# Experts' gate and up products as seven block products of halves, side by side in column halves of TensorE

## The chip, the cores and the metric

The kernel runs on one core of one Trainium2 chip. The metric is the device time of one execution in microseconds; a median of several runs is given. All data is float32. TensorE, VectorE (DVE), ScalarE (ACT), GpSimd (POOL) and SyncE (SP, here the issuer of most DMAs) run side by side and wait for each other by semaphores.

## What is computed

The network has two blocks; the second one has two layers, and each layer ends in a mixture of experts. Only that part is touched:

```python
def ec_moe(h, w_router, w_gate, w_up, w_down):
    n, d = h.shape[1], h.shape[2]
    cap = max(1, EC_FACTOR * n // N_EXPERTS)
    aff = jax.nn.softmax((h @ w_router).astype(jnp.float32), axis=-1)
    gate, idx = lax.top_k(jnp.swapaxes(aff, 1, 2), cap)
    xe = jax.vmap(lambda hb, ib: hb[ib])(h, idx)
    hid = jax.nn.silu(jnp.einsum('becd,edf->becf', xe, w_gate)) * jnp.einsum('becd,edf->becf', xe, w_up)
    ye = jnp.einsum('becf,efd->becd', hid, w_down) * gate[..., None].astype(h.dtype)
    return jax.vmap(lambda yb, ib: jnp.zeros((n, d), yb.dtype).at[ib.reshape(-1)].add(yb.reshape(-1, d)))(ye, idx)
```

n = 1024 tokens, d = f = 1024, 16 experts, cap = 128: each expert picks 128 tokens, so all its products are 128 x 1024 by 1024 x 1024. There are 16 experts in each of two layers, 32 in all, each with 12.6 MB of weights that are used once.

## The kernel before

P = 128, KD = 8 (blocks of 128 along d), BANK = 512 (the columns of one PSUM bank of float32). `ffn` sets up a layer's experts: `stage_route` makes the lists of tokens, and while it runs SyncE loads the first expert's gate and up weights (`ahead`). `stage_moe` then goes over the experts, two in one turn of a loop; `e` is the expert and `q` its parity.

One expert in `stage_moe`. GpSimd gathers the 128 rows of x by an indirect DMA into `xg[q]`, two experts ahead. TensorE turns them by eight transposes (`turn_x`, L2645) into PSUM banks 0 and 1, and VectorE and ScalarE write half of them each, scaled and shifted, to `xT` (`evac_x`, L2724 and L2696). TensorE makes gate and up in two column halves of 512: four products of 8 k steps (L2663), into banks 2 to 5; `xT[:, k, :]` is the stationary operand, the weights move. A float32 matmul appears as two LDWEIGHTS and two MATMUL instructions in the trace, so 32 of them are 64 rows. ScalarE takes Silu of a gate half (L2704), VectorE multiplies the up half onto it (L2737, to `sg`). TensorE turns h by eight transposes (`turn_h`, L2651); VectorE copies one half (L2739) and ScalarE the other (L2708) to `hT`. The turn of the next expert's x stands between the two halves of h. Then come two down products of 8 k steps (L2679) into banks 6 and 7; VectorE scales them (L2749) into `ye[q]`, and GpSimd adds them to the rows of `xacc` by an indirect DMA (L2637).

The order on each engine is written out by hand; each works its list strictly in order. SyncE's list loads six weight blocks of 2 MB an expert (L2601), each into its only buffer as soon as the product that read it is done: gate and up halves, then the down halves. So at any time the transfers run one expert ahead of TensorE.

What the prediction's steps touch elsewhere: the router's product (L2497) with two tiles of 32 columns, attention's value product (L3916) with two tiles of 64 columns, and the stages that already work by the seven products (`SEVEN`; L2291, L2840, L3082), whose sums VectorE makes.

## Time and profile before

| | us |
|---|---|
| median of 3 runs | 4650.78 |
| lowest, highest | 4643.99, 4653.27 |
| the profiled execution's own time | 4645.05 |
| its span, first to last instruction | 4643.3 |
| TensorE busy | 4159.4 |
| VectorE busy | 1900.6 |
| mean granted TensorE clock (share of full speed) | 0.949 |

In the rows below PE is a TensorE matmul, PEld a TensorE weight load. A timeline row has the start in us from the span's beginning, the length in us, and the number of instructions merged in it (x64); their last one ends with the row. Behind it may stand how long the engine was idle before and what ended that. "128*64 128x512" is a matmul with 128 rows and 64 columns of stationary operand and 512 moving columns. PEclk is the granted clock: 1.00 is 2.4 GHz, 0.50 is 1.2 GHz. In groups by line the numbers are: busy us in total, mean ns of one, then the idle time before them and what ended it.

### The profile page before, as it was taken

What the parts mean: (1) busy time and instruction counts of PE and PEld (TensorE: products, weight loads), DVE (VectorE), ACT (ScalarE), POOL (GpSimd) and SP (SyncE); (2) the same over time, 40 slices, a digit from 0 to 9 for tenths busy, and PEclk for the clock granted to TensorE, in tenths of its full rate; (3) what the DMA queues carried; (4) which work ended last, traced back from release to release, by engine and by line L of the source; (5) the groups of instructions that cost most, each with busy time, mean ns of one, the idle gap of its engine ahead of it and who ended that gap; (6) DMA issues with size and microseconds to landing.
All of it is one profiled execution on the core that took longest, in us unless ns stands there. A gap on an engine that the chain in (4) does not pass through costs nothing. (4 is left out here: it accounts for less than half of the span.)

```text
span 4643.3 us, 37101 instructions
## 1 busy us (share of the span) xinstructions
PE 4159.4 (90%) x13298; PEld 2120.7 (46%) x13298; DVE 1900.6 (41%) x3452; ACT 1011.0 (22%) x1952; POOL 361.5 (8%) x349
## 2 busy tenths in 40 slices
PE   8999998988889699785849999998999995999996
PEld 3444444683444454445424444444444542444442
DVE  3556555445757333455761111115656564111111
ACT  3434452343020311272120000003210111000001
POOL 1011010200000000182000000000000000000000
PEclk9999999999999899898879999998999997999998
DMA  5121216447444222007239999952011115999985
GB/s 113 53 64 65 72 57 206 142 118 249 146 149 154 65 69 69 5 1 206 63 133 362 316 314 322 317 193 91 25 50 70 50 39 221 342 315 324 317 310 195
DMA packets 524366, 739.72 MB, mean 159 GB/s; under 512 B 127574, under 2 KB 233910, under 8 KB 524216
## 3 DMA queue, kind: packets, MB, share of 16 engines
q1 hardware_dynamic: 499272, 687.45, 43.9%
q0 software_dynamic: 11744, 43.00, 3.3%
q10 hardware_dynamic: 13200, 7.34, 0.5%
q8 instruction: 86, 1.41, 0.1%
q14 instruction: 64, 0.52, 0.0%
HBM read 660.65 MB, written 77.06 MB: 159 GB/s over the span
## 5 line engine op out<-in xcount | busy, mean ns | idle before, releaser
L2663 PE MATMUL ps<-ffn_w,moe_xT 128*128 128x512 f32 x2048 | 888.6, 594 | 3.3 <-DVE moe_xT L2724 3.3
L2663 PEld LDWEIGHTS ps<-ffn_w,moe_xT 128*128 128x128 f32 x2048 | 390.7, 191 | 495.5 <-issue 491.5
L507 PE MATMUL ps<-hT,pr_w 128*128 128x512 f32 x1344 | 588.6, 595 | 5.1 <-issue 3.8
L2679 PE MATMUL ps<-moe_w,moe_hT 128*128 128x512 f32 x1024 | 444.9, 592 | 0.1
L507 PEld LDWEIGHTS ps<-hT,pr_w 128*128 128x128 f32 x1344 | 254.3, 191 | 319.7 <-issue 316.8
L2737 DVE TENSOR_TENSOR moe_sg<-moe_sg,ps 128x512 f32<-128x512 f32 x64 | 44.0, 688 | 837.7 <-PE ps L2663 837.7
L2679 PEld LDWEIGHTS ps<-moe_w,moe_hT 128*128 128x128 f32 x1024 | 192.1, 190 | 230.1 <-issue 230.1
L2704 ACT ACTIVATE moe_sg<-ps 128x512 f32<-128x512 f32 x64 | 38.2, 597 | 1008.0 <-PE ps L2663 1008.0
L3326 PE MATMUL ps<-hA,abp_w 128*128 128x512 f32 (+1 forms) x624 | 252.3, 565 | 0.6 <-DVE bv L3439 0.6
L2749 DVE SCALAR_TENSOR_TENSOR moe_ye<-ps,moe_gc,moe_gt 128x512 f32<-128x512 f32 x64 | 48.1, 751 | 388.4 <-PE ps L2679 388.4
L3326 PEld LDWEIGHTS ps<-hA,abp_w 128*128 128x128 f32 x624 | 118.2, 190 | 130.6 <-issue 127.8
L2637 POOL DMA_INDIRECT scratch_xacc<-moe_ye,idx x32 | 50.7, 1585 | 1250.2 <-DVE moe_ye L2749 1250.2
L2354 DVE TENSOR_TENSOR X<-X,ps 128x512 f32<-128x512 f32 x192 | 118.2, 681 | 36.5 <-PE ps L2303 35.3
L2077 PE MATMUL ps<-ple_w,mix 128*128 128x512 f32 x256 | 120.7, 627 | 6.0 <-DMA ple_w<-in_ple_w_gate 6.0
L3992 POOL TENSOR_SCALAR attn_Sc<-attn_Sc,attn_rd 128x640 f32<-128x640 f32 (+1 forms) x64 | 116.6, 1842 | 103.7 <-DVE attn_rd L3973 103.7
L2696 ACT ACTIVATE moe_xT<-ps,mod,gains 128x128 f32<-128x128 f32 x128 | 48.1, 456 | 327.1 <-PE ps L2645 327.1
L887 DVE TENSOR_SCALAR pr_cv<-pr_raw,pr_gw 128x1024 f32<-128x1024 f32 x24 | 20.0, 832 | 163.3 <-ACT pr_raw L673 163.2
L673 ACT ACTIVATE pr_raw<-ps 128x512 f32<-128x512 f32 x56 | 33.4, 596 | 243.9 <-PE ps L507 243.9
L1287 PE MATMUL ps<-hT,gdn_room 128*128 128x512 f32 x192 | 85.0, 592 | 0.0
L1977 DVE SCALAR_TENSOR_TENSOR ple_modacc<-ple_modw,cond,ple_modacc 128x512 f32<-128x512 f32 x112 | 81.7, 750 | 5.5
L3276 PE MATMUL ps<-abp_w,hA 128*128 128x512 f32 x160 | 72.1, 604 | 11.9 <-DMA abp_w<-in_ab_w_in 11.9
L2840 PE MATMUL ps<-gmv_sumB,gmv_sumA 128*128 128x512 f32 x192 | 82.7, 592 | 0.0
(680 smaller groups left out, 5813.9 us busy)
## 6 DMA issues: line engine op xcount, KB each, us to landing
ffn_w<-in_moe_w_gate SPq DMA_DIRECT2D x64, 2048.0 KB, 8.2
ffn_w<-in_moe_w_up SPq DMA_DIRECT2D x64, 2048.0 KB, 8.2
moe_w<-in_moe_w_down SPq DMA_DIRECT2D x64, 2048.0 KB, 10.5
wout_w<-in_w_mod SPq DMA_DIRECT2D x48, 512.0 KB, 3.9
ple_modw<-in_w_mod SPq DMA_DIRECT2D x48, 512.0 KB, 4.7
pr_w<-in_w_in SPq DMA_DIRECT2D x21, 1024.0 KB, 5.7
X<-scratch_grow SPq DMA_DIRECT2D x48, 256.0 KB, 6.3
X<-scratch_k SPq DMA_DIRECT2D x32, 256.0 KB, 5.2
```

The lines of the kernel that those rows point to most:

```text
L507: ins = eng.matmul(C.ps[r % NRING][:, :], w[:, (n // 2) % NW, k, (n % 2) * P:(n % 2 + 1) * P], HT[:, k, half * BANK:(half + 1) * BANK], st ...
L1287: ins = eng.matmul(C.ps[6 + half][:, :], zw[i // 2 % 2][:, k, (i % 2) * P:(i % 2 + 1) * P], HT[:, k, half * BANK:(half + 1) * BANK], start ...
L1977: ins = eng.scalar_tensor_tensor(a, w, c, a, ALU.mult, ALU.add)
L2077: ins = eng.matmul(C.ps[(u % nq) * ns + i][:, :], LT[:, k, t * P:(t + 1) * P], ws[i][:, c % ws[i].shape[1], k, :], start=(k == 0), stop=(k ...
L2354: eng.tensor_tensor(h, h, bank(p, t), ALU.add if sg > 0 else ALU.subtract).then_inc(s_acc, 1)
L2637: eng.indirect_dma_start(xacc, bass.IndirectOffsetOnAxis(ap=idx[:, e:e + 1], axis=0), ye[e % 2][:, :], None, compute_op=ALU.add).then_inc( ...
L2663: ins = eng.matmul(C.ps[2 + b][:, :], xT[:, k, :], wb[b][:, k, :], start=(k == 0), stop=(k == KD - 1))
L2679: ins = eng.matmul(C.ps[6 + half][:, :], hT[:, k, :], wb[4 + half][:, k, :], start=(k == 0), stop=(k == KD - 1))
L2840: ins = eng.matmul(bank(q, t), left[:, t * P:(t + 1) * P], right, start=(k == 0), stop=(k == K2 - 1))
L3276: ins = eng.matmul(C.ps[v % 6][:, :], HA[:, k, t * P:(t + 1) * P], w[:, 0, k, :], start=(k == 0), stop=(k == KD - 1))
L3326: ins = eng.matmul(C.ps[4 * (n % 2) + bank][:, 0:wd], w[:, buf[kind], k, i * P:(i + 1) * P], HA[:, k, col:col + wd], start=(k == 0), stop= ...
L3992: ins = eng.tensor_scalar(Sc[q][:, g, h, lo:], Sc[q][:, g, h, lo:], rd[q][:, i:i + 1], None, ALU.mult)
```

## The change

Gate and up of an expert are made by seven block products in place of eight (Winograd's form of Strassen's scheme). x is cut into two halves of 64 tokens (`LO`, `HI`) and two halves of k (QK = 4 blocks); the weights into two halves of k and two of columns, "11", "12", "21", "22". With S1 = x21 + x22, S2 = S1 - x11, S3 = x11 - x21, S4 = x12 - S2 and T1 = w12 - w11, T2 = w22 - T1, T3 = w22 - w12, T4 = w21 - T2 the products are P1 = x11 w11, P2 = x12 w21, P3 = S4 w22, P4 = x22 T4, P5 = S1 T1, P6 = S2 T2, P7 = S3 T3, and the four quarters of the result are P1+P2, P1+P6+P5+P3, P1+P6+P7+P4, P1+P6+P7+P5.

- TensorE: each product has 64 rows of result, so gate goes to partitions 0 to 63 of a bank and up to 64 to 127, by `tile_position` 0 and 64. The order is P3, P1, P6, P2, P5, P7, turn of the next x, first half of P4, turn of h's upper half, rest of P4, then the down product by k halves with the turn of h's lower half in it.
- VectorE: the weight sums are written over the weights, 16 operations of 128x1024 an expert (`wsum`); the T1 sums of the next expert come at the end of an expert's list (`first_sum`). The products are joined by operations of 512 that read PSUM.
- GpSimd: the four x sums of 128x256 (`sums`).
- ScalarE: a copy of P1, Silu in three pieces, half of `hT`, half of x.
- SyncE: quarters are loaded when the product or sum that last read them is done; "22" and the down weights have two sets of buffers, the second in rooms that were free in this stage (the router's input tile `room`, and `X`). Total bytes are the same.
- `xT` has one buffer still, so x of the next expert is written only when P4 is done.

The core of the diff:

```diff
+QK = KD // 2
+
+
+def quarter(W, b):
+    h, c = int(b[0]) - 1, int(b[1]) - 1
+    return W[:, h * QK * P:(h + 1) * QK * P, c * BANK:(c + 1) * BANK]
...
+        wd0 = [st.sb(f"wd{h}", [P, QK, D]) for h in two]
...
+        XS = room[:, 0, :].rearrange("p (s k t) -> p s k t", s=4, k=QK)
+        R0, R1 = room[:, 1, 0:BANK], room[:, 1, BANK:2 * BANK]
+        U, R2 = room[:, 2, :], room[:, 7, 0:BANK]
...
+            def load_down(e, q):
+                for h in (1, 0):
+                    eng.dma_start(down(q, h), wd[bass.ds(e, 1), h * QK * P:(h + 1) * QK * P, :].rearrange("a (k p) c -> p (a k) c", p=P)).then_inc(s_d[q][h], 16)
+
+            def load_quarter(e, q, b):
+                for m in two:
+                    src = quarter(GU[m], b)[bass.ds(e, 1)].rearrange("a (k p) c -> p (a k) c", p=P)
+                    if b == "11" or (b == "22" and q):
+                        for c in (1, 0):
+                            eng.dma_start(piece(b, m, q, c).rearrange("p (k c) -> p k c", k=2), src[:, 2 * c:2 * c + 2, :]).then_inc(s_w[b][q], 16)
+                    else:
+                        eng.dma_start(wq[b][m][:, :, :], src).then_inc(s_w[b][q], 16)
+
+            def expert(e, q, later):
+                if later:
+                    eng.wait_ge(s_T, 16 * e - 16)
+                load_quarter(e, q, "22")
+                eng.wait_ge(s_p5, e)
+                load_quarter(e, q, "12")
+                eng.wait_ge(s_p7, e)
+                load_quarter(e, q, "11")
+                eng.wait_ge(s_p4, e)
+                load_quarter(e, q, "21")
+                if later:
+                    eng.wait_ge(s_y, 2 * e - 2)
+                else:
+                    eng.wait_ge(s_xs, 16 * NT)
+                load_down(e, q)
...
+            def sums(e):
+                x11, x12, x21, x22 = xT[:, 0:QK, LO], xT[:, QK:KD, LO], xT[:, 0:QK, HI], xT[:, QK:KD, HI]
+                eng.wait_ge(s_xv, e + 1)
+                eng.wait_ge(s_xa, e + 1)
+                eng.tensor_tensor(XS[:, 0, :, :], x21, x22, ALU.add).then_inc(s_S, 1)
+                eng.tensor_tensor(XS[:, 2, :, :], x11, x21, ALU.subtract).then_inc(s_S, 1)
+                eng.wait_ge(s_S, 4 * e + 1)
+                eng.tensor_tensor(XS[:, 1, :, :], XS[:, 0, :, :], x11, ALU.subtract).then_inc(s_S, 1)
+                eng.wait_ge(s_S, 4 * e + 3)
+                eng.tensor_tensor(XS[:, 3, :, :], x12, XS[:, 1, :, :], ALU.subtract).then_inc(s_S, 1)
...
+                if e + 1 < E:
+                    sums(e + 1)
...
+            def product(x, bank, b, q, sums=None, ks=range(QK)):
+                for k in ks:
+                    if sums is not None and k % 2 == 0:
+                        eng.wait_ge(s_T, sums + 2 + k)
+                    for m in two:
+                        ins = eng.matmul(C.ps[bank][TH * m:TH * (m + 1), :], XL[x](k), rows(b, m, q, k),
+                                         start=(k == 0), stop=(k == QK - 1), tile_position=(0, TH * m))
+                return ins
...
+                eng.wait_ge(s_S, 4 * e + 4)
+                eng.wait_ge(s_w["22"][q], i * 64 + 64 if q else i * 32 + 32)
+                product(3, 3, "22", q).then_inc(s_p3, 1)
+                eng.wait_ge(s_w["11"][q], e * 64 + 32)
+                product(1, 2, "11", q).then_inc(s_p1, 1)
+                product(6, 4, "22", q, sums=16 * e + 4).then_inc(s_p6, 1)
+                eng.wait_ge(s_w["21"][q], e * 32 + 32)
+                product(2, 5, "21", q).then_inc(s_p2, 1)
+                eng.wait_ge(s_sp1, e + 1)
+                product(5, 2, "12", q, sums=16 * e).then_inc(s_p5, 1)
+                eng.wait_ge(s_u2, e + 1)
+                product(7, 4, "11", q, sums=16 * e + 8).then_inc(s_p7, 1)
                 if not last:
                     turn_x(i + q, 1 - q)
-                turn_h(e, 1)
+                eng.wait_ge(s_u11, e + 1)
+                product(4, 5, "21", q, sums=16 * e + 12, ks=(0, 1))
+                eng.wait_ge(s_hh, e + 1)
+                for k in range(QK):
+                    ins = eng.transpose(C.ps[3][:, k * P:(k + 1) * P], sg[:, BANK + k * P:BANK + (k + 1) * P], C.ident[:, :])
+                ins.then_inc(s_ht1, 1)
+                product(4, 5, "21", q, sums=16 * e + 12, ks=(2, 3)).then_inc(s_p4, 1)
                 if later:
                     eng.wait_ge(s_y0, e)
                     eng.wait_ge(s_y1, e)
-                for half in range(2):
-                    eng.wait_ge(s_w[4 + half], e * 16 + 16)
-                    for k in range(KD):
-                        if half == 0 and k == 0:
-                            eng.wait_ge(s_hv, e + 1)
-                        if half == 0 and k == 4:
-                            eng.wait_ge(s_ha, e + 1)
-                        ins = eng.matmul(C.ps[6 + half][:, :], hT[:, k, :], wb[4 + half][:, k, :], start=(k == 0), stop=(k == KD - 1))
-                    ins.then_inc(s_y, 1)
+                eng.wait_ge(s_d[q][1], i * 16 + 16)
+                eng.wait_ge(s_ha, e + 1)
+                down_half(q, 1, 0)
+                eng.wait_ge(s_hl, e + 1)
+                for k in range(QK):
+                    ins = eng.transpose(C.ps[2][:, k * P:(k + 1) * P], sg[:, k * P:(k + 1) * P], C.ident[:, :])
+                ins.then_inc(s_ht0, 1)
+                down_half(q, 1, 1)
+                eng.wait_ge(s_d[q][0], i * 16 + 16)
+                eng.wait_ge(s_hv, e + 1)
+                for half in two:
+                    down_half(q, 0, half).then_inc(s_y, 1)
...
+                eng.wait_ge(s_p1, e + 1)
+                eng.activation(R0, C.ps[2][:, :], ACT.Copy).then_inc(s_sp1, 1)
+                eng.wait_ge(s_g11, e + 1)
+                eng.activation(sg[LO, 0:BANK], sg[LO, 0:BANK], ACT.Silu).then_inc(s_si11, 1)
+                eng.wait_ge(s_gh, e + 1)
+                eng.activation(sg[:, BANK:2 * BANK], sg[:, BANK:2 * BANK], ACT.Silu).then_inc(s_sih, 1)
+                eng.wait_ge(s_ht1, e + 1)
+                eng.activation(flat(hT[:, QK:KD, :]), C.ps[3][:, :], ACT.Copy).then_inc(s_ha, 1)
+                eng.wait_ge(s_g21, e + 1)
+                eng.activation(sg[HI, 0:BANK], sg[HI, 0:BANK], ACT.Silu).then_inc(s_si21, 1)
                 if not last:
-                    evac_x(i + q, 1 - q)
-                eng.wait_ge(s_ht, e * 2 + 2)
-                eng.activation(hT[:, 4:8, :].rearrange("p k c -> p (k c)"), C.ps[hbank[1]][:, :], ACT.Copy).then_inc(s_ha, 1)
-
-            evac_x(0, 0)
-            expert(0, 0, False, False)
-            expert(0, 1, False, False)
+                    evac_x(i + q, 1 - q, e)
...
+            def wsum(q, out, a, b, c):
+                for m in two:
+                    eng.tensor_tensor(piece(out, m, q, c), piece(a, m, q, c), piece(b, m, q, c), ALU.subtract).then_inc(s_T, 1)
+
+            def first_sum(i, q):
+                e = i * 2 + q
+                eng.wait_ge(s_w["12"][q], e * 32 + 32)
+                eng.wait_ge(s_w["11"][q], e * 64 + 32)
+                for c in two:
+                    wsum(q, "12", "12", "11", c)
+
             def expert(i, q, later, last):
                 e = i * 2 + q
+                eng.wait_ge(s_T, 16 * e + 4)
+                eng.wait_ge(s_p3, e + 1)
+                for c in two:
+                    wsum(q, "22", "22", "12", c)
+                eng.wait_ge(s_T, 16 * e + 8)
+                eng.wait_ge(s_p1, e + 1)
+                for c in two:
+                    wsum(q, "11", "22", "11", c)
+                eng.wait_ge(s_p6, e + 1)
+                eng.wait_ge(s_sp1, e + 1)
+                eng.tensor_tensor(R2, R0, C.ps[4][:, :], ALU.add).then_inc(s_u2, 1)
+                eng.wait_ge(s_p2, e + 1)
+                eng.tensor_tensor(sg[LO, 0:BANK], R0[LO, :], C.ps[5][LO, :], ALU.add).then_inc(s_g11, 1)
+                eng.tensor_tensor(U[LO, 0:BANK], R0[HI, :], C.ps[5][HI, :], ALU.add).then_inc(s_u11, 1)
+                for c in two:
+                    wsum(q, "21", "21", "22", c)
+                eng.wait_ge(s_u11, e + 1)
+                eng.wait_ge(s_si11, e + 1)
+                eng.tensor_tensor(sg[LO, 0:BANK], sg[LO, 0:BANK], U[LO, 0:BANK], ALU.mult).then_inc(s_c11, 1)
+                eng.wait_ge(s_p5, e + 1)
+                eng.wait_ge(s_u2, e + 1)
+                eng.tensor_tensor(R1, R2, C.ps[2][:, :], ALU.add).then_inc(s_v5, 1)
+                eng.wait_ge(s_v5, e + 1)
+                eng.tensor_tensor(sg[LO, BANK:2 * BANK], R1[LO, :], C.ps[3][LO, :], ALU.add)
+                eng.tensor_tensor(U[LO, BANK:2 * BANK], R1[HI, :], C.ps[3][HI, :], ALU.add)
+                eng.wait_ge(s_p7, e + 1)
+                eng.tensor_tensor(sg[HI, BANK:2 * BANK], R1[LO, :], C.ps[4][LO, :], ALU.add).then_inc(s_gh, 1)
+                eng.tensor_tensor(U[HI, BANK:2 * BANK], R1[HI, :], C.ps[4][HI, :], ALU.add).then_inc(s_c22, 1)
+                eng.tensor_tensor(R2, R2, C.ps[4][:, :], ALU.add).then_inc(s_u3, 1)
+                eng.wait_ge(s_c22, e + 1)
+                eng.wait_ge(s_sih, e + 1)
+                eng.tensor_tensor(sg[:, BANK:2 * BANK], sg[:, BANK:2 * BANK], U[:, BANK:2 * BANK], ALU.mult).then_inc(s_hh, 1)
+                eng.wait_ge(s_p4, e + 1)
+                eng.wait_ge(s_u3, e + 1)
+                eng.tensor_tensor(sg[HI, 0:BANK], R2[LO, :], C.ps[5][LO, :], ALU.add).then_inc(s_g21, 1)
+                eng.tensor_tensor(U[HI, 0:BANK], R2[HI, :], C.ps[5][HI, :], ALU.add).then_inc(s_u21, 1)
+                eng.wait_ge(s_u21, e + 1)
+                eng.wait_ge(s_si21, e + 1)
+                eng.tensor_tensor(sg[HI, 0:BANK], sg[HI, 0:BANK], U[HI, 0:BANK], ALU.mult).then_inc(s_hl, 1)
+                if not last:
+                    evac_x(i + q, 1 - q, e)
+                eng.wait_ge(s_ht0, e + 1)
+                eng.tensor_copy(flat(hT[:, 0:QK, :]), C.ps[2][:, :]).then_inc(s_hv, 1)
+                if not last:
+                    first_sum(i + q, 1 - q)
```

## Rows read from the trace of the kernel before

**Rows 1.** The page, section 1: busy time of each engine, share of the span, instructions.
```profile
PE 4159.4 (90%) x13298; PEld 2120.7 (46%) x13298; DVE 1900.6 (41%) x3452; ACT 1011.0 (22%) x1952; POOL 361.5 (8%) x349
```
**Rows 2.** Busy time by stretch: from and to, length, then engines, clock, DMA, GB/s.
```profile
core 0: us, PE busy (x) PEld busy (x) DVE busy (x) ACT busy (x) POOL busy (x), PEclk, DMA share, GB/s
2480.00:2900.00 420.00, 420.00 (x1100) 195.18 (x1099) 48.35 (x99) 31.83 (x70) 25.75 (x20) 1.00 0.93 322
```
**Rows 3.** Timeline of TensorE over one expert and into the next: start, length, merged instructions.
```profile
2995.26 27.63 PE L2663 MATMUL ps<-ffn_w,moe_xT 128*128 128x512 f32 x64
3022.73 0.60 PE L2651 MATMUL ps<-ident,moe_sg 128*128 128x128 f32 x4
...
3024.47 13.90 PE L2679 MATMUL ps<-moe_w,moe_hT 128*128 128x512 f32 x32
3038.21 27.63 PE L2663 MATMUL ps<-ffn_w,moe_xT 128*128 128x512 f32 x64
```
**Rows 4.** Column tiles in the router (L2497) and attention (L3916): timeline, then L3916's loads.
```profile
2378.65 1.88 PE L2497 MATMUL ps<-hA,route_wr 128*32 128x512 f32 x8
...
2011.42 1.09 PE L3906 MATMUL ps<-ident,attn_Sc 128*128 128x128 f32 x8
2012.44 1.08 PE L3916 MATMUL ps<-attn_PT,bv 128*64 128x512 f32 x4
2013.45 0.92 PE L3884 MATMUL ps<-bk,bq 64*128 64x384 f32 x4
...
L3916 PEld LDWEIGHTS ps<-attn_PT,bv x152: 132/134/137, 1973.3 to 2090.7; 128*64 128x64 f32 x152
```
**Rows 5.** Timeline of VectorE elsewhere: operations of 1024, of 512, of 64 partitions.
```profile
1073.83 2.35 DVE L1857 TENSOR_TENSOR mix<-mix,outs_gz 128x1024 f32<-128x1024 f32 x2
1076.10 1.22 DVE L1862 TENSOR_TENSOR outs_y<-outs_y,outs_z 128x1024 f32<-128x1024 f32 x1
...
1134.72 4.87 DVE L2354 TENSOR_TENSOR X<-X,ps 128x512 f32<-128x512 f32 x8
...
2380.59 0.68 DVE L2526 COPY route_lgT<-ps 64x512 f32<-64x512 f32 x1 [12.18 <-PE ps L2497]
```
**Rows 6.** The same expert's VectorE (timeline), and ScalarE's Silu (groups by line).
```profile
3022.93 0.69 DVE L2737 TENSOR_TENSOR moe_sg<-moe_sg,ps 128x512 f32<-128x512 f32 x1 [13.05 <-PE ps L2663]
...
L2704 ACT ACTIVATE moe_sg<-ps 128x512 f32<-128x512 f32 x64 | 38.2, 597 | 1008.0 <-PE ps L2663 1008.0
```
**Rows 7.** GpSimd: its sum of 256 (groups by line), and beside VectorE (timeline).
```profile
L1186 POOL TENSOR_TENSOR gdn_M<-gdn_M,gdn_tmp 128x256 f32<-128x256 f32 x1 | 0.7, 733 | 0.1
...
314.01 1.59 POOL L473 TENSOR_TENSOR pr_QQ<-pr_QQ,pr_qt 128x512 f32<-128x512 f32 x1
314.51 1.64 DVE L958 TENSOR_TENSOR pr_ik<-pr_fr,pr_ft 128x512 int32<-128x512 f32 x1
```
**Rows 8.** Timeline of the first expert layer's start.
```profile
2432.41 1.36 DVE L2724 TENSOR_SCALAR moe_xT<-ps,gains,mod 128x128 f32<-128x128 f32 x4 [8.09 <-PE ps L2645]
...
2434.01 30.54 PE L2663 MATMUL ps<-ffn_w,moe_xT 128*128 128x512 f32 x64 [1.64 <-DVE moe_xT L2724]
```
**Rows 9.** DMA from 3000 to 3043 us in 40 slices; the page, section 6, weight loads.
```profile
GB/s 366 303 250 229 225 389 406 408 402 389 389 385 387 387 387 385 242 402 410 402 392 191 74 368 406 406 398 297 2 0 101 362 404 392 402 290 59 211 412 379
...
ffn_w<-in_moe_w_gate SPq DMA_DIRECT2D x64, 2048.0 KB, 8.2
```
**Rows 10.** Timeline of GpSimd: the gather of a later expert's rows.
```profile
2784.14 0.99 POOL L2624 DMA_INDIRECT moe_xg<-scratch_xrows,idx  x1 [0.30 <-issue]
```
**Rows 11.** Two idles of TensorE in other stages (timeline), and the stretches around them.
```profile
3628.41 7.11 PE L3082 MATMUL ps<-gmu_sumA,vG 128*128 128x512 f32 x16 [1.78 <-DVE gmu_sumA L3129]
3622.00:3632.00 10.00, 8.22 (x46) 5.91 (x46) 6.09 (x11) 0.00 (x0) 0.00 (x0) 1.00 0.00 0
...
3503.76 8.41 PE L2291 MATMUL ps<-gmo_firstw,gmo_sumA 128*128 128x512 f32 x14 [5.42 <-DVE gmo_sumA L2335]
3501.30:3508.00 6.70, 4.24 (x5) 1.85 (x6) 5.68 (x10) 0.00 (x0) 0.00 (x0) 0.50 0.72 249
```

More of the change, by code:

```diff
@@ L2646, in turn_x, with down_half @@
                 ins.then_inc(s_xt[q], 1)
[L2648 to L2652 removed]
+            def product(x, bank, b, q, sums=None, ks=range(QK)):
[6 more added lines that the diff above has]
+                return ins
+            def down_half(q, h, half):
+                for k in range(QK):
+                    ins = eng.matmul(C.ps[6 + half][:, :], hT[:, QK * h + k, :], down(q, h)[:, k, half * BANK:(half + 1) * BANK],
+                                     start=(h == 1 and k == 0), stop=(h == 0 and k == QK - 1))
+                return ins
             def expert(i, q, later, last):
```

114 lines of the change are left out of this document (53 added, 61 removed).

## Prediction

> **What bounds the kernel now.** The page comes first: TensorE is busy for 90% of the span and no other engine for half of it [rows 1]. The change touches only the expert layers, so the next view is a stretch of one of them: in 420 us TensorE is busy for all 420 at the full clock, VectorE for 48, ScalarE for 32, and the DMA engines are busy for 93% [rows 2]. TensorE is the bound and DMA the second. The order of TensorE's work in one expert [rows 3] gives the period that all further terms are held against: from one expert's first matmul to the next one's 3038.21 - 2995.26 = 42.95 us. In it 64 gate and up matmuls take 3022.73 - 2995.26 = 27.47 us, that is 0.429 us each; 32 down matmuls take 13.74; sixteen 128-wide transposes take 1.74, or 0.11 each. Nothing in it waits. There are 32 such periods (16 experts in each of two layers), some 1,374 us of the 4,643.
>
> **What the change takes away.** A float32 matmul is two instructions of one slot (0.429 us) each. Before, gate and up are 4 products x 8 k x 2 = 64 slots. After, each of the seven products has 4 k steps, and each step gate and up (2 x 2 instructions), on 64 stationary columns each. If both run at once, a product is 8 slots (3.43 us) and the seven are 56. So 8 slots go: 3.43 us an expert.
>
> Do two column halves run at once? The router's products have this form (two column tiles, each its own moving operand of 512): the last 8 instructions stand in 1.88 us, (1.88 - 0.59) / 3 = 0.43 for each pair. With 64 columns, as in the change, attention's four instructions run from 2012.44 to the next matmul at 2013.45: 1.01 us, two slots of 0.43 and 0.15, where four in turn would need 1.72 [rows 4]. I take the full pairing.
>
> A rule speaks against it. The weight load of 64 columns lasts 134 ns, and in the router's steady stretch the spacing stays 0.43, so the loads hide behind the other tile's matmuls [rows 4]. The Trainium skill (TensorE: Matmul & The Clock Gate, "Part 3: Packing small matmuls") says that a weight load overlaps running matmuls only where the row group differs; the change's two tiles have all rows in common. By that rule each slot would grow by its load (a rival below); by the row it doesn't, and the row has the same row group.
>
> **What it adds on TensorE.** The array changes between whole and halved form six times an expert: into product 3, out to the eight x transposes, into product 4, out to four h transposes, back in, out to the down product. Attention's change out is the 0.15 above; eight transposes there take 2012.44 - 2011.42 = 1.02 where 8 x 0.11 = 0.88, so 0.14 for the way in [rows 4]. Six times 0.15 is 0.9 us. Without waits the period is 42.95 - 3.43 + 0.9 = 40.4 us. The bounds of one change are 0.05 and 0.25, so 39.8 to 41.0.
>
> **What it adds on VectorE, and the new wait.** Sixteen in-place sums of 128x1024 an expert. Such an operation lasts 1.22 us and two in a row 2.35, so 1.13 apart. A 128x512 operation lasts 0.69, and eight in a row 4.87, so 0.60 apart; 64 partitions cost the same: the router's 64x512 copy lasts 0.68 [rows 5]. TensorE's result reaches VectorE or ScalarE 0.2 us after its last slot (27.47 + 0.2 against 3022.93 - 2995.26 = 27.67) [rows 3, 6]. A result handed over starts its reader 0.04 after it ends (matmuls until 3022.89, VectorE 3022.93), which I use inside VectorE too; a Silu on ScalarE lasts 0.60 [rows 6]. VectorE's order, from product 3's first slot as zero (product ends: 3.5, 6.9, 10.4, 13.8, 17.2, 20.65):
> - w22 sums start at 3.7 (they overwrite what product 3 reads); four end at 8.35. Product 6 needs the first pair (6.1) at 6.9 and the second at 8.6, so it has 0.2 us to spare.
> - w11 sums wait for them: 8.4 to 13.0. P1 + P6 at 12.9.
> - Product 2's end (13.8 + 0.2): two 512 operations, then the w21 sums from 15.2; the last starts at 18.6. Product 7 (w11 sums, 13.0, needed 17.2) and product 4 (w21 sums, 17.6, needed 21.8) don't wait.
> - From 19.8 eight operations of 512: h11's product, P1+P6+P5 (its reader waits until it ends, 0.1 more), two with P3, three with P7, and at 24.1 the product that gives h's upper half (its Silu ends before, at 23.6). It ends at 24.8.
> TensorE is there earlier: products to 20.65, x transposes to 21.7, half of product 4 from 21.8 to 23.5, change of form to 23.6. The h transposes wait until 24.8: **a new wait of 1.2 us** in each expert. Period 40.4 + 1.2 = 41.6. Behind that wait stand product 4's other half and all of the down product. The rest of VectorE's list has room: h's lower half ends at 29.5 and is needed at 30.8; the x evacuation, the copy of h and the first sums of the next expert (32 to 37) end before the next 41.6; ScalarE has some 5 us of work between.
> Gain: 42.95 - 41.6 = 1.33 us an expert, times 32 = **42.6 us**.
>
> **GpSimd and the layer's start.** Four 128x256 sums of x an expert move onto GpSimd, 0.73 us each [rows 7]. In the loop they lie beside the down product (from 30.9, 10.8 us of cover; product 3 of the next expert waits for them if it is gone), also where they take turns with VectorE's sums (4 x 0.73 + 4 x 1.22 = 7.8). The turns are what the trace shows: a 128x512 VectorE operation with two SBUF inputs lasts 1.64 instead of 0.69 where a GpSimd operation (1.59) began 0.5 us before it [rows 5, 7]. The Trainium skill (SBUF — State Buffer, "SBUF: two separate sides") calls this an exclusive lock for the whole instruction; the row agrees. At a layer's start there is no cover: matmuls began at 2434.01, right behind the evacuation of x (2432.41 and 1.36 us) [rows 8]; now the four sums on GpSimd come between, beside VectorE's first weight sums, which start at the same time. Alone 4 x 0.73 and hand-offs, 3.2; taking turns up to 8. I take 7, since the trace shows turns: twice 7 = **14 us lost**.
>
> **DMA, queues.** The bytes stay. Six loads of 2,048 KB (12.6 MB) must pass in 41.6 instead of 42.95 us, 3% faster; one expert's window reaches over 400 GB/s in many slices and has slices near zero [rows 9], so the engines have room. SyncE's list: w12 after product 5, w11 after product 7, then w21, down and the next w22 together after product 4: 8.4 MB, some 21 us at 400 GB/s, of which the first 2 MB are needed 24 us later, and down and w22 are double buffered. w12 and w11, issued at 17.4 and 20.85, are needed by the first sums at 32; a load of 2 MB lands in 8.2 us [rows 9]. I cost this at nothing; a late load would only eat VectorE's slack behind 32. GpSimd's gather (0.99 us) starts 2784.14 - (3038.21 - 6 x 42.95) = 3.6 us after an expert's first matmul [rows 3, 10] and now meets the w22 sums. No row shows such a meeting: between 0 and 0.8 us of delay there. Product 6's slack takes 0.2, so 0 to 0.6 on the period. I take 0, for a descriptor job is nearer to a DMA than to rows 7's tensor operation.
>
> **Sum.** 42.6 - 14 = 28.6 us. The profiled execution (4645.05) would become 4616.4; it lies 5.7 us under the median of the runs, 4650.78, and the forecast is made for the median: **4622 us**, 0.6% faster. Own range 4600 to 4641.
>
> **Rivals.**
> 1. *No stall* (VectorE's list a little shorter than added up, or the switches cheaper): 32 x 2.5 = 80 less 6 to 14: 4577 to 4585. For it: 1.2 us is only 5% of VectorE's list. Against: every term has its row. 10%.
> 2. *VectorE later*: gather against w22 sums (+0.6 x 32 = 19 us, 4641) or each of its 23 operations up to the wait 25 to 40 ns longer, through waits on its own results and register work: 0.6 to 0.9 us an expert, 4641 to 4651. 18%.
> 3. *The wait costs the clock* (slower). Each expert now has an idle of 1.2 us in TensorE's work, with transposes around it. An idle of 1.78 us before L3082 left the granted clock at 1.00, one of 5.42 before L2291 brought it to 0.50 [rows 11]. If it falls in the experts, a price is the layer's start: 64 matmuls in 30.54 instead of 27.63 us, 2.9 us [rows 3, 8]. It decides from 0.9 us an expert (28.6 / 32), so a fall in one expert of three is enough; in each it gives 4622 + 93 = 4715, in two of three 4684. 9%.
> 4. *Weight loads not hidden* (the rule above): 56 x 0.134 = 7.5 us more, while the 1.2 us wait goes: period 47.9, 32 x 5.0 + 14: 4825. The router's row stands against it. 4%.
> 5. *Halves run in turn*, so that it doesn't do what it says: 112 slots, 4622 + 32 x 22.8 = 5352. Rows 4 exclude it nearly. 1%.
> 6. A layer start or order effect that I don't see, 4641 to 4680: 8%.
>
> **Chances.** Forecast's own range 50%, the rivals as given (10, 18, 9, 4, 1, 8). Range: from inside rival 1, 4580, to 4675, which takes in 2, most of 6 and little of 3. A measurement of this kernel can tell about 0.2% (9.3 us) from no change. Faster than 4641.5: 50 + 10 + a few of 2 = 63%. Within: rival 2's rest and a part of 6, 18%. Slower: 3, 4, 5 and the rest, 19%.
>
> **What would show it.** Right: periods of 41.6 us; product pairs 0.43 apart; a wait of 1.2 us before the h transposes, released by VectorE's product, and none before product 6; first product 3 some 7 us later than 2434.01 less what came before it; clock 1.00 in the layers. Wrong: a wait at product 6 (rival 2), a clock under 1.00 (3), slots over 0.43 (4), or DMA as a releaser of TensorE or VectorE.

## The result and the profile after

The changed kernel takes 4670.48 us (median of 6 runs, 4667.3 to 4676.17) against 4651.18 for the kernel before, run beside it (6 runs, 4643.99 to 4653.27). The ratio is 1.0046, 95% interval 1.0033 to 1.0059: **slower by 0.46%**, where 4622 and faster was forecast. The time lies inside the range (4580 to 4675), but the sign is wrong.

The page of the changed kernel, section 1, its execution of 4671.63 us with a span of 4669.9 (before: [rows 1]), and one row of the view by stretch, over some 13 experts of the first layer (before: [rows 2]). Its columns are those of [rows 2].

```profile
PE 4112.2 (88%) x14834; PEld 1988.5 (43%) x14834; DVE 2784.3 (60%) x4348; ACT 1055.6 (23%) x2016; POOL 506.0 (11%) x477
...
2480.00:3060.00 580.00, 555.64 (x2145) 210.44 (x2145) 435.70 (x509) 59.97 (x119) 96.24 (x83) 0.98 0.88 319
```

TensorE was busy without a gap before; now 24.4 of 580 us are idle, and the granted clock is 0.98 instead of 1.00. VectorE went from 12% of such a stretch to 75%. The timeline of TensorE shows where the 24 us are; here through the second half of one expert (start, length, instruction, and in brackets the idle time before it and its releaser). The two halves alternate, so each matmul has a line of its own.

```profile
2639.75 1.09 PE L2704 MATMUL ps<-ident,moe_xg 128*128 128x128 f32 x8
2640.77 0.64 PE L2712 MATMUL ps<-ffn_w21g,moe_xT 128*64 128x512 f32 x1
2640.78 0.64 PE L2712 MATMUL ps<-ffn_w21u,moe_xT 128*64 128x512 f32 x1
2641.25 0.59 PE L2712 MATMUL ps<-ffn_w21g,moe_xT 128*64 128x512 f32 x1
2641.26 0.59 PE L2712 MATMUL ps<-ffn_w21u,moe_xT 128*64 128x512 f32 x1
2641.68 0.59 PE L2712 MATMUL ps<-ffn_w21g,moe_xT 128*64 128x512 f32 x1
...
2644.58 0.66 PE L2744 MATMUL ps<-ident,moe_sg 128*128 128x128 f32 x4 [1.87 <-DVE moe_sg L2862]
...
2645.94 1.06 PE L2712 MATMUL ps<-ffn_w21g,moe_xT 128*64 128x512 f32 x1
...
2646.79 1.06 PE L2712 MATMUL ps<-ffn_w21g,moe_xT 128*64 128x512 f32 x1
...
2648.65 3.74 PE L2718 MATMUL ps<-moe_wd,moe_hT 128*128 128x512 f32 x8
```

Three things stand here. Gate and up matmuls start in pairs, 0.43 us from pair to pair (2641.25 to 2641.68): the column halves do run at once. Ahead of the four h transposes (L2744) TensorE waits 1.87 us for VectorE's product L2862. And behind this wait the pairs stand 0.85 apart (2645.94 to 2646.79) instead of 0.43. The view by stretch says why, for that part and for the one ahead of the wait:

```profile
2641.00:2644.50 3.50, 1.71 (x8) 0.29 (x4) 3.41 (x6) 0.63 (x1) 0.00 (x0) 1.00 1.05 393
2645.34:2648.75 3.41, 3.41 (x9) 0.61 (x7) 0.00 (x0) 0.53 (x1) 0.00 (x0) 0.50 1.05 387
```

For 3.41 us the granted clock is 0.50, the 1.2 GHz level. Such a stretch is called a fall of the clock from here on, and the experts in which it happens are said to fall. 13 of the 32 do, six in the first layer and seven in the second; their periods are 44.06 us, those of the undisturbed ones 42.41 (42.95 before, [rows 3]).

The rest of the loss stands at the layer's start (timeline; before: [rows 8]):

```profile
2439.12 1.36 DVE L2814 TENSOR_SCALAR moe_xT<-ps,gains,mod 128x128 f32<-128x128 f32 x4 [8.30 <-PE ps L2704]
2440.41 1.21 DVE L2820 TENSOR_TENSOR ffn_w12g<-ffn_w12g,ffn_w11g 128x1024 f32<-128x1024 f32 x1
2440.78 4.83 POOL L2675 TENSOR_TENSOR hA<-moe_xT 128x256 f32<-128x256 f32 x1 [5.90 <-ACT moe_xT L2779]
...
2443.81 1.22 DVE L2820 TENSOR_TENSOR ffn_w12u<-ffn_w12u,ffn_w11u 128x1024 f32<-128x1024 f32 x1
2445.57 0.72 POOL L2676 TENSOR_TENSOR hA<-moe_xT 128x256 f32<-128x256 f32 x1
...
2448.03 1.08 PE L2712 MATMUL ps<-ffn_w22g,hA 128*64 128x512 f32 x1 [8.94 <-POOL hA L2680]
```

From the end of x's evacuation (2440.48) to the first matmul it now takes 7.55 us; before it was 2434.01 - 2433.77 = 0.24. So 7.3 us each, in both layers.

**The account**, from the two profiled executions, whose own times differ by 4671.63 - 4645.05 = 26.6 us. The end of x's evacuation came 6.7 us later (2440.48 against 2433.77), in stages that the change doesn't touch; the run b4wait below, which has the kernel before in all these stages, had its first expert matmul at 2440.92 instead of 2434.01, so two executions can differ by this much without the change. The layers' starts cost 14.6. The experts of the first layer took 689.24 us instead of 689.63, those of the second 692.53 instead of 688.3: together +3.8. That is 25.1; 1.5 lie between and after the layers. Without the 6.7 the change costs some 20 us, as the medians say (19.3). The experts' +3.8 is a gain and a loss: 32 x (42.95 - 42.41) = 17.3 us less for the shorter period, 13 x 1.65 = 21.5 more for the falls of the clock, less 0.4 for the rest (the first expert of each layer among it).

### The profile page after: what moved, and what is told of

Same layout as the page of the kernel before. It is cut to its first block and busy times, and to the rows that moved or that the text cites. A ratio compares the mean times of both kernels' runs of the same rounds, so it can differ in the third digit from the quotient of the medians.

```text
span 4669.9 us, 42435 instructions
## 1 busy us (share of the span) xinstructions
PE 4112.2 (88%) x14834; PEld 1988.5 (43%) x14834; DVE 2784.3 (60%) x4348; ACT 1055.6 (23%) x2016; POOL 506.0 (11%) x477
## 5 line engine op out<-in xcount | busy, mean ns | idle before, releaser
L2712 PE MATMUL ps<-ffn_w21u,moe_xT 128*64 128x512 f32 x512 | 255.2, 634 | 0.0
L2712 PE MATMUL ps<-ffn_w21g,moe_xT 128*64 128x512 f32 x512 | 255.1, 633 | 0.0
L2718 PE MATMUL ps<-moe_wd,moe_hT 128*128 128x512 f32 x512 | 230.1, 603 | 0.0
L2718 PE MATMUL ps<-X,moe_hT 128*128 128x512 f32 x512 | 228.0, 598 | 0.0
L2718 PEld LDWEIGHTS ps<-moe_wd,moe_hT 128*128 128x128 f32 x512 | 96.6, 194 | 128.8 <-issue 128.8
L2718 PEld LDWEIGHTS ps<-X,moe_hT 128*128 128x128 f32 x512 | 95.5, 192 | 123.9 <-issue 123.9
L2712 PE MATMUL ps<-ffn_w11u,moe_xT 128*64 128x512 f32 x256 | 115.1, 592 | 0.0
L2712 PE MATMUL ps<-ffn_w11g,moe_xT 128*64 128x512 f32 x256 | 115.1, 592 | 0.0
L2820 DVE TENSOR_TENSOR ffn_w12g<-ffn_w12g,ffn_w11g 128x1024 f32<-128x1024 f32 x64 | 96.9, 1513 | 0.0
L2820 DVE TENSOR_TENSOR ffn_w12u<-ffn_w12u,ffn_w11u 128x1024 f32<-128x1024 f32 x64 | 93.5, 1461 | 0.0
```

The lines of the kernel that those rows point to most:

```text
L2712: ins = eng.matmul(C.ps[bank][TH * m:TH * (m + 1), :], XL[x](k), rows(b, m, q, k), start=(k == 0), stop=(k == QK - 1), tile_position=(0, T ...
L2718: ins = eng.matmul(C.ps[6 + half][:, :], hT[:, QK * h + k, :], down(q, h)[:, k, half * BANK:(half + 1) * BANK], start=(h == 1 and k == 0), ...
L2820: eng.tensor_tensor(piece(out, m, q, c), piece(a, m, q, c), piece(b, m, q, c), ALU.subtract).then_inc(s_T, 1)
```

## The experiments

Each is a kernel with one edit, beside new runs of the kernel before (medians 4648.6 to 4651.3). "Period" is from one expert's first matmul to the next one's, without a fall of the clock.

**order: VectorE's list ahead of the multiply made shorter.** The edit, in VectorE's expert():

```diff
-                eng.tensor_tensor(sg[LO, 0:BANK], sg[LO, 0:BANK], U[LO, 0:BANK], ALU.mult).then_inc(s_c11, 1)
 ...
-                eng.tensor_tensor(R2, R2, C.ps[4][:, :], ALU.add).then_inc(s_u3, 1)
 ...
                 eng.tensor_tensor(sg[:, BANK:2 * BANK], sg[:, BANK:2 * BANK], U[:, BANK:2 * BANK], ALU.mult).then_inc(s_hh, 1)
+                eng.tensor_tensor(sg[LO, 0:BANK], sg[LO, 0:BANK], U[LO, 0:BANK], ALU.mult).then_inc(s_c11, 1)
+                eng.tensor_tensor(R2, R2, C.ps[4][:, :], ALU.add).then_inc(s_u3, 1)
```

(The first one's two waits move with it.)

> VectorE's product of the h11 quarter (0.71 us with its start-to-start distance) and its second sum into R2 (0.61 us) are moved behind the multiply that TensorE's four h transposes wait for; nothing else changes. Theory A (the new wait is VectorE's list of work before that multiply, and the falls of the granted clock are what follows that wait): the wait goes from 1.95 to about 0.6 us, the period of an undisturbed expert from 42.41 to about 41.1, no expert or only a few fall to 0.50, and the time is 4670.5 - 32 x 1.32 - 13 x 1.65 = about 4607 us. Rival B (the clock falls because products of half columns load the array otherwise, whatever the wait): the period is 41.1, but some 13 experts still fall: about 4628 us. Rival C (something else ends last, such as ScalarE's Silu of the same half): the period stays above 42: about 4665 us.

Measured: 4610.98 us (4 runs), ratio to before 0.991 (0.9894 to 0.9927). Period 41.23, no expert falls. The wait is 0.69 us where 0.6 was expected. Theory A holds, within 4 us of its 4607; B and C fall. This order alone turns a loss of 0.46% into a gain of 0.9%, with the same work.

**start: GpSimd's sums ahead of VectorE's at the layer's start.**

```diff
             evac_x(0, 0, None)
+            eng.wait_ge(s_S, 4)
             first_sum(0, 0)
```

> VectorE waits for GpSimd's four first sums before it begins its own four at the start of an expert layer; nothing else changes. Theory A (GpSimd's first sum took 4.83 us because VectorE's sums ran back to back beside it, and it is what TensorE's first matmul waits for): GpSimd's four sums take 0.72 us each, the gap before the first matmul of a layer goes from 7.5 to about 3.2 us, VectorE's own sums begin 3 us later and are still done long before the product that needs them (they are due some 13 us behind the first matmul): 2 x 4.3 = 8.6 us less, about 4662 us. Rival (GpSimd's first sum is slow by itself, or waits for its weights): the gap stays at 7.5 us or grows, no gain, 4670 us.

Measured: 4661.05 us (10 runs), ratio to before 1.0018 (1.0008 to 1.0027), 9.4 less than the changed kernel. The timeline of its first layer's start:

```profile
2441.76 0.72 POOL L2675 TENSOR_TENSOR hA<-moe_xT 128x256 f32<-128x256 f32 x1 [5.78 <-ACT moe_xT L2779]
2442.44 0.72 POOL L2676 TENSOR_TENSOR hA<-moe_xT 128x256 f32<-128x256 f32 x1
...
2444.90 1.08 PE L2712 MATMUL ps<-ffn_w22g,hA 128*64 128x512 f32 x1 [4.84 <-POOL hA L2680]
```

The same sum takes 0.72 us instead of 4.83 and the gap from x's evacuation (2440.10 and 1.36) to the first matmul is 3.4 us instead of 7.55. The periods of the experts are those of the changed kernel (42.41 and 44.06, 12 falls instead of 13). Theory A holds.

**whole: are 64 partitions dearer than 128?** Seven operations of VectorE work on all 128 partitions (three of them also write elsewhere, and h gets other values). The edit, by two of them:

```diff
-                eng.tensor_tensor(sg[HI, BANK:2 * BANK], R1[LO, :], C.ps[4][LO, :], ALU.add).then_inc(s_gh, 1)
-                eng.tensor_tensor(U[HI, BANK:2 * BANK], R1[HI, :], C.ps[4][HI, :], ALU.add).then_inc(s_c22, 1)
+                eng.tensor_tensor(sg[:, BANK:2 * BANK], R1[:, :], C.ps[4][:, :], ALU.add).then_inc(s_gh, 1)
+                eng.tensor_tensor(U[:, BANK:2 * BANK], R1[:, :], C.ps[4][:, :], ALU.add).then_inc(s_c22, 1)
```

> VectorE's seven operations on 64 partitions ahead of the multiply of the upper half work on all 128 partitions instead (three of them also write elsewhere), which changes the values of h: the output is not the reference's. Theory A (an operation that follows one of 64 partitions starts only when that has ended, 0.71 us instead of 0.60): the seven now stand 0.60 apart, the multiply ends 0.7 to 0.8 us earlier, the wait before the h transposes is 1.2 us and the period 41.7 us. Rival (the distance comes from what they read or from their order, not from the 64 partitions): still 0.71 us, wait 1.95, period 42.4.

Measured: 4627.47 us (one run). First the changed kernel's VectorE ahead of the multiply (timeline; L2862 is the multiply), then the same lines of whole:

```profile
3031.98 0.68 DVE L2854 TENSOR_TENSOR moe_sg<-hA,ps 64x512 f32<-64x512 f32 x1
3032.68 0.69 DVE L2855 TENSOR_TENSOR hA<-hA,ps 64x512 f32<-64x512 f32 x1
3033.38 0.68 DVE L2857 TENSOR_TENSOR moe_sg<-hA,ps 64x512 f32<-64x512 f32 x1
3034.09 0.69 DVE L2858 TENSOR_TENSOR hA<-hA,ps 64x512 f32<-64x512 f32 x1
3034.81 0.69 DVE L2859 TENSOR_TENSOR hA<-hA,ps 128x512 f32<-128x512 f32 x1
3035.42 0.68 DVE L2862 TENSOR_TENSOR moe_sg<-moe_sg,hA 128x512 f32<-128x512 f32 x1
```
```profile
2972.51 0.69 DVE L2854 TENSOR_TENSOR hA<-hA,ps 128x512 f32<-128x512 f32 x1
2973.11 0.68 DVE L2855 TENSOR_TENSOR moe_sg<-hA,ps 128x512 f32<-128x512 f32 x1
2973.71 0.68 DVE L2857 TENSOR_TENSOR moe_sg<-hA,ps 128x512 f32<-128x512 f32 x1
2974.31 0.68 DVE L2858 TENSOR_TENSOR hA<-hA,ps 128x512 f32<-128x512 f32 x1
2974.91 0.68 DVE L2859 TENSOR_TENSOR hA<-hA,ps 128x512 f32<-128x512 f32 x1
2975.50 0.68 DVE L2862 TENSOR_TENSOR moe_sg<-moe_sg,hA 128x512 f32<-128x512 f32 x1
```

The lengths are the same, 0.68 to 0.69. The starts are not: after an operation on 64 partitions the next one starts 0.70 to 0.72 later, when it has ended; after one on 128 it starts 0.60 later, while the first still drains. The period is 41.62, the forecast's 41.6; no expert falls. Theory A holds, and the time is what was forecast for the changed kernel, 5 us off.

**v3 and v4: both edits, and the last wait taken away.** v3 is order and start together, and the last of the four w21 sums goes behind the multiply as well (the third goes between the operations with P3 and those with P7):

```diff
-                for c in two:
-                    wsum(q, "21", "21", "22", c)
+                wsum(q, "21", "21", "22", 0)
 ...
+                eng.tensor_tensor(piece("21", 0, q, 1), piece("21", 0, q, 1), piece("22", 0, q, 1), ALU.subtract).then_inc(s_T, 1)
                 eng.wait_ge(s_p7, e + 1)
 ...
                 eng.tensor_tensor(sg[:, BANK:2 * BANK], sg[:, BANK:2 * BANK], U[:, BANK:2 * BANK], ALU.mult).then_inc(s_hh, 1)
+                eng.tensor_tensor(piece("21", 1, q, 1), piece("21", 1, q, 1), piece("22", 1, q, 1), ALU.subtract).then_inc(s_T, 1)
```

> The two edits above together, and one step more: of the four in-place sums of the w21 weights that VectorE makes ahead of the multiply, the last (1.14 us) goes behind it. Theory A (VectorE's list alone makes the wait, the wait makes the clock falls): the multiply would end about 2.46 us earlier, before TensorE comes to it, so its wait goes to nothing or to 0.2 us for the moved sum; the period is about 40.5 us, the granted clock stays at 1.00 within the experts, and the time is 4670.5 - 32 x 1.9 - 13 x 1.65 - 8.6 = about 4580 us, 70 us below the kernel before. Rival B (the falls belong to the products of half columns): period 40.5, but experts still fall, about 4600 us. Rival C (another work takes the place of the wait): period near 42, about 4650 us.

Measured: 4585.53 us (4 runs), ratio to before 0.9858 (0.9842 to 0.9875), 5.5 above the expected 4580. No expert falls; period 40.77. The groups of TensorE from 2480 to 3060 us (name, shape, count, then busy time and mean, then idle time before them and its releaser) show that the wait before the h transposes is gone and 0.23 us (3.2 over 14) of a new one are left, for the moved sum:

```profile
L2712 PE MATMUL ps<-ffn_w21g,moe_xT 128*64 128x512 f32 x224 | 104.4, 598 | 3.2 <-DVE ffn_w21u L2859 3.2
...
L2744 PE MATMUL ps<-ident,moe_sg 128*128 128x128 f32 x56 | 9.2, 286 | 0.0
```

v4 splits that sum by k step:

```diff
-                eng.tensor_tensor(piece("21", 1, q, 1), piece("21", 1, q, 1), piece("22", 1, q, 1), ALU.subtract).then_inc(s_T, 1)
+                eng.tensor_tensor(piece("21", 1, q, 1)[:, 0:BANK], piece("21", 1, q, 1)[:, 0:BANK], piece("22", 1, q, 1)[:, 0:BANK], ALU.subtract).then_inc(s_T, 1)
+                eng.tensor_tensor(piece("21", 1, q, 1)[:, BANK:2 * BANK], piece("21", 1, q, 1)[:, BANK:2 * BANK], piece("22", 1, q, 1)[:, BANK:2 * BANK], ALU.subtract).then_inc(s_T2, 1)
 ... (TensorE)
-                product(4, 5, "21", q, sums=16 * e + 12, ks=(2, 3)).then_inc(s_p4, 1)
+                product(4, 5, "21", q, sums=16 * e + 12, ks=(2,))
+                eng.wait_ge(s_T2, e + 1)
+                product(4, 5, "21", q, ks=(3,)).then_inc(s_p4, 1)
```

> The kernel with the three edits of the run v3, in which TensorE still waited 0.24 us in each expert for the last w21 sum before k step 2 of product 4. That sum of 128x1024 is split into its two k steps of 128x512, and TensorE waits for the second only before k step 3. Theory A (nothing else ends later): the first half is there 0.53 us earlier, the wait goes, the period falls from 40.77 to about 40.5, and the time is 4585.5 - 32 x 0.24 = about 4578 us. Rival (VectorE's list is 0.06 us longer and product h11 and R2 then come too late for h21, or the wait only moves to k step 3): 4585 us or more.

Measured: 4579.68 us (4 runs), ratio 0.985 (0.9834 to 0.9867). Period 40.47, and no idle of TensorE is left in the experts. **v4 is the fastest kernel of this study**, 1.5% under the kernel before; against v3 its gain of 5.9 us is near the expected 7.5, but the kernel before was itself 2.6 us faster beside it, and their intervals overlap; what shows the gain is the period, 0.30 shorter. Its 40.47 is the first direct measurement of the period without waits (forecast: 40.4), and the measure for what a wait costs in the others.

**longer, mid, w16, w13: how long may the wait be?** These change only the length of the wait, up or down. longer, w16 and mid put operations whose results nobody reads ahead of the multiply; w16 moves h11's product behind it, mid h11's product and the sum into R2, w13 the sum into R2 alone. The edits of longer, mid, w16 and w13, in this order:

```diff
+                eng.tensor_tensor(U[:, 0:BANK], R1, R1, ALU.add)
+                eng.tensor_tensor(R0, R1, R1, ALU.add)
 ... mid, on top of order:
+                eng.tensor_tensor(R0, R1, R1, ALU.add)
+                eng.tensor_tensor(U[HI, 0:256], R1[HI, 0:256], R1[HI, 0:256], ALU.add)
 ... w16 (h11's product moved as in order):
+                eng.tensor_tensor(U[HI, 0:256], R1[HI, 0:256], R1[HI, 0:256], ALU.add)
 ... w13:
-                eng.tensor_tensor(R2, R2, C.ps[4][:, :], ALU.add).then_inc(s_u3, 1)
 ... (behind the multiply)
+                eng.tensor_tensor(R2, R2, C.ps[4][:, :], ALU.add).then_inc(s_u3, 1)
```

> The changed kernel with two additional operations of 128x512 whose results nobody reads ahead of the multiply: the wait before the h transposes goes from 1.95 to about 3.15 us. Theory A (the wait makes the falls, a longer one more of them or longer ones): undisturbed period 43.6, falls in more than 13 experts, 4670.5 + 32 x 1.2 = 4709 us and more, up to 4709 + 19 x 1.65 = 4740 us. Rival B (falls come from the products, not from the wait): again 13 falls, 4709 us.

> The order with the two operations moved behind the multiply, and in their place two operations whose results nobody reads (one of 128x512, one of 64x256) ahead of it: a wait of TensorE between the 1.2 us and the 1.95 us of the other runs, about 1.7 us, with none of the products or values changed. Theory A (the length of the wait decides whether the clock falls, with the bound between 1.2 and 1.95 us): period about 42.2; falls in some experts or in none, which sets the bound on one side of 1.7 us. If falls: some 10 x 1.65 us more than 4611 + 32 x 1.0 = 4643, so 4660; if none 4643. Rival (the order of VectorE's work matters, not the wait): no falls at any wait in this order.

> The changed kernel with the product of h11 (0.71 us) moved behind the multiply of h's upper half, and an operation of 64x256 whose result nobody reads (about 0.4 us) ahead of it: a wait of TensorE of about 1.6 us, between the 1.2 us at which no expert fell and the 1.84 us at which 11 of 32 did. Theory A (falls begin with the length of the wait): period 42.1; either a few experts fall (4670.5 - 32 x 0.3 - 13 x 1.65 = 4639, plus 1.65 for each) or none (4639).

> The changed kernel with the second sum into R2 alone (0.61 us) moved behind the multiply: a wait of about 1.3 us, with the output of the reference. Theory A: no expert falls, period 41.8, and the time is 4670.5 - 32 x 0.61 - 13 x 1.65 = about 4630 us, so that a change of one line in the order of VectorE's work turns slower than before into faster than before. Rival (1.3 us is enough for a fall in some experts): 4630 plus 1.65 us for each.

**b4wait: the same wait in the kernel before.** Does it need the new products for the clock to fall?

```diff
+        junk = st.sb("junk", [P, 4, HB], mybir.dt.bfloat16)
 ...
                     eng.wait_ge(s_si, e * 2 + half + 1)
+                    if half == 1:
+                        for r in range(4):
+                            eng.tensor_tensor(junk[:, r, :], sg[:, 1, :], sg[:, 1, :], ALU.add)
                     eng.tensor_tensor(sg[:, half, :], sg[:, half, :], C.ps[3 + 2 * half][:, :], ALU.mult).then_inc(s_h, 1)
```

> The kernel before, without block products, but with four additional VectorE operations of 128x512 (0.60 us apart, into a tile that nobody reads) ahead of the multiply of the second half of h, for which TensorE's second set of h transposes waits: TensorE gets a wait of about 1.9 us in each expert that it did not have, as long as in the changed kernel, but all its products fill the whole array. Theory A (the granted clock falls because of a wait of this length, whatever the products): the undisturbed period goes from 42.95 to about 44.8, and in some ten of the 32 experts the clock falls to 0.50, 1.65 us more each: 4651 + 32 x 1.9 + 16 = about 4728 us or more. Rival B (products of half columns are part of the cause): no expert falls, 4651 + 61 = 4712 us.

The group of the transposes that wait, in the same view and stretch as above, of order, w13, w16, the changed kernel, b4wait and longer, in this order (four instructions to a wait; some records are missing):

```profile
L2744 PE MATMUL ps<-ident,moe_sg 128*128 128x128 f32 x56 | 9.2, 287 | 9.7 <-DVE moe_sg L2858 9.7
```
```profile
L2744 PE MATMUL ps<-ident,moe_sg 128*128 128x128 f32 x52 | 8.5, 287 | 16.7 <-DVE moe_sg L2861 16.7
```
```profile
L2744 PE MATMUL ps<-ident,moe_sg 128*128 128x128 f32 x52 | 8.5, 287 | 23.9 <-DVE moe_sg L2860 23.9
```
```profile
L2744 PE MATMUL ps<-ident,moe_sg 128*128 128x128 f32 x52 | 8.5, 287 | 24.4 <-DVE moe_sg L2862 24.4
```
```profile
L2652 PE MATMUL ps<-ident,moe_sg 128*128 128x128 f32 x96 | 15.1, 280 | 22.5 <-DVE moe_sg L2741 22.5
```
```profile
L2744 PE MATMUL ps<-ident,moe_sg 128*128 128x128 f32 x48 | 11.4, 379 | 36.9 <-DVE moe_sg L2864 36.9
```

In b4wait only four of every eight transposes wait, so its 22.5 us are 12 waits. With the periods and the experts in which the clock falls to 0.50 (counted over both layers; the idle is that of the other 30 experts, for the last one of each layer has no next x to turn and waits longer, 3.05 us in the changed kernel):

| kernel | idle at one wait, us | period, us | experts that fall | time, us |
|---|---|---|---|---|
| v4 | 0 | 40.47 | 0 | 4579.7 (4 runs) |
| order | 0.69 | 41.23 | 0 | 4611.0 (4 runs) |
| whole | 1.09 | 41.62 | 0 | 4627.5 (1 run) |
| w13 | 1.28 | 41.83 | 0 | 4634.2 (1 run) |
| w16 | 1.84 | 42.38 | 13 | 4667.6 (1 run) |
| mid | 1.84 | 42.37 | 13 | 4671.8 (1 run) |
| the changed kernel | 1.88 | 42.41 | 13 | 4670.5 (6 runs) |
| longer | 3.08 | 43.61 | 26, seven of them for 6.83 us | 4736.6 (1 run) |
| b4wait | 1.88 | 45.32 (before: 42.95) | 17 | 4760.9 (2 runs) |

A single run gives a time to a few us only (the six runs of the changed kernel span 9); the waits, periods and falls of these kernels are each from one trace.

What follows. The falls depend on the length of the wait that comes back in each expert: of the 30 experts with the wait of the table, none falls up to 1.28 us, 11 (mid, w16) and 13 (the changed kernel) at 1.84 to 1.88, 24 at 3.08. mid has order's sequence with two operations more, and falls where order doesn't, so it isn't the sequence. w13 has the changed kernel's work, every product of it, with the wait 0.6 us shorter, and doesn't fall. And b4wait has none of the half-column products and falls more often than the changed kernel with an idle of the same length. Theory A holds and B falls: **the wait makes the clock fall, whatever the products**. Its length doesn't decide alone, though. The last expert of each layer waited 1.87 us in order, 2.26 in whole, 2.47 in w13 and 3.05 in the changed kernel, and in none of these eight cases did the clock fall; in mid and w16 it fell in all four, at 3.01. Nor does any run take away the transposes on both sides of the wait, so their part in it is not tested.

Some expectations missed in size. w16 was to have a wait of 1.6 us and had 1.84, the same as mid: its operation of 64x256 cost 0.72 + 0.44 - 0.60 = 0.56 us instead of 0.4 (see the last section), and the sum into R1 started 1.25 behind the last w21 sum where h11's product had started 1.13 behind it; so nothing was measured between 1.28 and 1.84, and with 13 falls the time is 4667.6 where 4639 + 13 x 1.65 = 4660 was expected. mid missed its 4660 in the same way: 1.84 instead of 1.7, and 13 falls instead of ten; 4611 + 32 x (42.37 - 41.23) + 13 x 1.65 = 4669, measured 4671.8. b4wait was to take some 4728 us. Its wait cost 2.37 us a period instead of 1.9: the waiting transposes start 2.04 later in the expert than before (30.82 against 28.78 behind its first matmul), the down product comes 0.70 behind them instead of 0.43, and 0.06 are lost in it. 17 falls instead of ten at 1.70 us make 29: 4651 + 76 + 29 = 4756, with 5 more unexplained. (Where an expectation above speaks of 11 falls at 1.84 us in mid, the last expert of each layer was not yet counted; with it they are 13.)

## Why the prediction was wrong, step by step

- **The products.** Pairs 0.43 us apart, 3.43 a product, eight slots gone: right. The six changes of the array's form at 0.15: v4's period without waits is 40.47 where 40.4 was worked out. The rule of the Trainium skill (TensorE: Matmul & The Clock Gate, "Part 3: Packing small matmuls"), by which a weight load hides only where the row group differs, and with it rival 4, fell: the tiles here have all rows in common and the pairs stand 0.43 apart, not 0.43 + 0.134. Rival 5 fell with it.
- **VectorE's list up to product 2's end.** Right: from product 3's first slot as zero, w22 sums at 3.7, w11 sums at 8.4, P1 + P6 at 12.9, h11's first operation at 14.0. No wait before product 6, so the gather cost nothing there, as taken.
- **The operations of 512 behind it: the first step that failed.** The sentence "64 partitions cost the same" read the row of a single 64x512 operation, 0.68 us [rows 5]. That is its length, and it is right. But the sum counts distances between starts, and the 0.60 came from a row of eight operations on 128 partitions. No row of 64-partition operations back to back had been looked for. Each costs 0.09 to 0.12 more. Two of them stand ahead of the w21 sums, which began 15.43 behind zero instead of 15.2, and five among the eight, which began at 19.98 instead of 19.8; the multiply ended at 25.53 instead of 24.8, and the wait became some 1.9 us instead of 1.2. Run whole shows it alone: period 41.62 against 42.41. That is 0.79 x 32 = 25 us of the miss.
- **The clock: rival 3, given 9%.** The mechanism was named; its point of decision was put by two idles of another kind (1.78 us without a fall, 5.42 with one, [rows 11]), so a wait of 1.2 looked safe. It is, as whole and w13 show. At the real wait of 1.88 it isn't, in 13 of 32 experts; the 1.78 us of [rows 11] stood alone, these come once in each 42 us. The price was put at 2.9 us an expert, measured are 1.65 (44.06 - 42.41); 13 of them are 21.5 us. The decision "from 0.9 us an expert" was not reached by the clock alone (21.5 / 32 = 0.67), but with the step above.
- **The two hang together.** With VectorE's list as added up, whole's 4627 would have come, beside the forecast's 4622. The mis-sized term cost 25 us itself and by pushing the wait past the length at which falls begin 21.5 more: 4622 + 25 + 21.5 = 4669, measured 4670.5.
- **The layer's start.** 7 us forecast, 7.3 measured. The mechanism was only near: the turns that [rows 7] led to would have let GpSimd in after each VectorE operation. Instead its first sum ended only behind all four of VectorE's (from 2440.78 to 2445.6), and the other three then took 0.72 each. The Trainium skill (SBUF — State Buffer, "SBUF: two separate sides") calls it an exclusive lock, held for the whole instruction; here GpSimd was kept out through four instructions in a row. That 7 was near 7.3 is in part luck, for it was chosen between 3.2 and 8. In the loop the turns came as forecast (last section).
- **DMA, queues.** Nothing, as taken: no wait of TensorE or VectorE in the experts ends with a DMA. The gather beside the w22 sums lasted 0.98 us (0.99 before, [rows 10]), and these began at 3.70 as added up.
- **The base.** Taking the forecast from the median, not from the profiled execution, was right: the stages ahead of the layers alone differed by 6.7 us between the two profiled executions.

## What to carry to other kernels

Where an engine that was nearly idle gets a long list beside the bound (here from 12% busy to 75%), the order of that list decides: look at each operation ahead of the one that the bound waits for, and move behind it whatever isn't needed yet. Here two moved operations were worth 60 us, three times what the change had lost, and with the further edits of v4 the same change went from 0.46% slower to 1.5% faster. In adding up such a list take distances between starts, from rows of the same number of partitions, not lengths; and look for a second price of a wait, through the clock: here a wait of TensorE of 1.8 us and more in each expert had one.
